# Casts and sigmoids placed behind bank copies, another order at the entry of the feed-forward stage, and 20 instead of 16 pairs in seven products

## The reference

```python
    x = x + merged @ wo
    h = rmsnorm(x, g_ffn)
    a, u = jnp.split(h @ w_gu, 2, axis=-1)
    return x + (jax.nn.silu(a) * u) @ w_dn
```

## Time and profile before

| | us |
|---|---|
| median of 3 runs | 1005.48 (1004.69 to 1010.24) |
| profiled execution, its time | 1006.62 |
| its span in the profile | 1004.5 |
| TensorE busy | 952.2 |
| VectorE busy | 602.9 |
| ScalarE busy | 403.2 |
| feed-forward stage, first product to last | 580.8 to 992.5 |

### The profile page before, as it was taken

How to read it: one execution, slowest core, us unless ns; L and a number is a source line. 1 busy time by engine, 2 the same in 40 slices (tenths; PEclk the granted TensorE clock), 3 DMA queues, 4 the chain that set the end, 5 groups by cost and what they waited for, 6 DMA issues and landing times. The chain is left out here.

```text
span 1004.5 us, 18642 instructions
## 1 busy us (share of the span) xinstructions
PE 952.2 (95%) x7431; PEld 926.3 (92%) x7431; DVE 602.9 (60%) x1167; ACT 403.2 (40%) x746; POOL 77.4 (8%) x107
## 2 busy tenths in 40 slices
PE   6999999999999899999999988999999899999997
PEld 5899989999988898999999977999999899999997
DVE  5745465445985661735355768876448776447653
ACT  7343234444553441422223545454225444225453
POOL 0100023011202000202031000000000000000000
PEclk9999999999999999999999979999999999999999
DMA  8783237322312774232222331524212313221302
GB/s 238 177 235 44 45 89 178 101 76 77 104 47 71 202 197 134 76 94 85 84 85 79 119 136 43 209 74 135 86 43 84 126 44 127 84 85 47 106 19 89
DMA packets 104912, 104.78 MB, mean 104 GB/s; under 512 B 11130, under 2 KB 101752, under 8 KB 104492
## 3 DMA queue, kind: packets, MB, share of 16 engines
q1 hardware_dynamic: 101224, 92.51, 30.9%
q0 software_dynamic: 3552, 11.08, 4.0%
q10 hardware_dynamic: 52, 0.01, 0.0%
HBM read 97.74 MB, written 15.45 MB: 113 GB/s over the span
## 5 line engine op out<-in xcount | busy, mean ns | idle before, releaser
L651 PE MATMUL acc<-h_hi,w_hi 128*128 128x288 f32 (+1 forms) x816 | 256.9, 315 | 3.1 <-DVE w_lo L634 2.1
L651 PE MATMUL acc<-h_lo,w_hi 128*128 128x288 f32 (+1 forms) x816 | 234.8, 288 | 0.0
L651 PE MATMUL acc<-h_hi,w_lo 128*128 128x288 f32 (+1 forms) x800 | 229.9, 287 | 0.0
L651 PEld LDWEIGHTS acc<-h_hi,w_hi 128*128 128x128 f32 x816 | 153.8, 188 | 11.7 <-issue 4.9
L651 PEld LDWEIGHTS acc<-h_lo,w_hi 128*128 128x128 f32 x816 | 154.0, 189 | 4.1 <-issue 2.4
L651 PEld LDWEIGHTS acc<-h_hi,w_lo 128*128 128x128 f32 x800 | 150.5, 188 | 0.0
L1366 PE MATMUL acc<-h_hi,w_hi 128*128 128x272 f32 x440 | 129.7, 295 | 15.5 <-ACT acc L1803 15.4
L624 ACT ACTIVATE w_hi<-raw 128x1024 fp32r<-128x1024 f32 (+1 forms) x67 | 70.5, 1052 | 166.1 <-PE acc L651 165.3
L1366 PE MATMUL acc<-h_lo,w_hi 128*128 128x272 f32 x440 | 128.8, 293 | 0.0
L1366 PE MATMUL acc<-h_hi,w_lo 128*128 128x272 f32 x440 | 128.7, 293 | 0.0
L1781 ACT ACTIVATE w_hi<-raw 128x512 fp32r<-128x512 f32 (+1 forms) x105 | 64.8, 621 | 97.5 <-PE acc L1366 91.9
(11 more groups left out here) (401 smaller groups left out, 1999.1 us busy)
## 6 DMA issues: line engine op xcount, KB each, us to landing
raw<-in_w_in SPq DMA_DIRECT2D x25, 1024.0 KB, 5.6
raw<-in_w_gate_up SPq DMA_DIRECT2D x22, 1024.0 KB, 5.2
raw<-in_w_down SPq DMA_DIRECT2D x8, 1024.0 KB, 5.3
rev<-tab POOLq DMA_DIRECT2D x1, 4352.0 KB, 20.2
ring<-in_cache_dsa_kv SPq DMA_DIRECT2D x4, 1024.0 KB, 7.8
raw<-in_w_out SPq DMA_DIRECT2D x4, 1024.0 KB, 5.8
out<-in_cache_dsa_kv SPq DMA_DIRECT2D x2, 2016.0 KB
ring<-in_cache_moba_k SPq DMA_DIRECT2D x48, 64.0 KB, 2.6
```

The source lines that it names most:

```text
L651: ins = nc.tensor.matmul(acc[:, bank, 0:HALF[half]], a[:, k, :], two(b[:, kx + k, :], half), start=first and k == k0 and c == 0, stop=last ...
```

## The change

- Of the 22 gate and up pairs only the first and the last stay in the eight-product form: 20 instead of 16 are in the seven-product form, pairs 1 to 8, 13 to 20 and 25 to 28.
- The sigmoids of a seven-form gate pair come at 3.1 products behind it in ScalarE's queue (1.8 before), those of pair 0 at 1.2; the casts of a seven-form up pair at 4.2 and 4.45 (1.5 and 1.75), their low parts on VectorE 0.8 behind; the gate multiplies at 3.7 (3.6).
- At the entry: the second norm's matmuls at product 9 instead of 2, its roots at 9.5 instead of 2.5, its reciprocal at 10.5 instead of 3.1, `over_rms` from 14.5 instead of 8.5 on. The high and low parts of h for q = 2 are made in two halves, the slots 4 to 7 later, and the sums and slots 4 to 7 of q = 3 later too. The first six weight operands have times of their own (`EARLY`).

```diff
-        EIGHT = (0, 4, 8, 13, 17, 21)
+        EIGHT = (0, 21)
...
-        RING, LEAD = 6, 5
+        RING = 6
+        EARLY = (n_wout - 1.6, n_wout - 1.55, n_wout - 0.95, n_wout - 0.9, n_wout + 1, n_wout + 1.75)
...
-            return tm(last_use[operands[u - RING]] + 1) if u >= RING else tm(u - LEAD) if u >= 4 else n_wout - 0.94 + 0.05 * u
+            return tm(last_use[operands[u - RING]] + 1) if u >= RING else EARLY[u]
...
-        T_SIG, T_GATE = 1.8, 3.6
+        T_SIG, T_GATE = 3.1, 3.7
...
-            return q + 1 if q < 3 else 4 + min(slot // 2, 2) if q == 3 else 6 + 2 * (q - 4) + (1 if slot < 2 else 2)
+            first = {0: (1, 1, 1), 1: (2, 2, 2), 2: (3, 3, 6), 3: (4, 5, 7)}
+            return first[q][min(slot // 2, 2)] if q < 4 else 7 + 2 * (q - 4) + (1 if slot < 2 else 2)
...
-            return lag(n, 1.5 + 0.25 * m_) if n in seven else tm(evac_time[n, "12" if m_ == 0 else "22"] + 0.3)
+            return lag(n, 4.2 + 0.25 * m_) if n in seven else tm(evac_time[n, "12" if m_ == 0 else "22"] + 0.3)
...
                 def second_norm():
-                    yield tm(2)
+                    yield tm(9)
...
-                    for q in range(3):
+                    for q in range(2):
                         yield n_merge + 2 * q + 2.5
                         act.wait_ge(sem("b_sum"), 4 * q + 4)
                         b_his(q, slice(0, 8), h8_hi[:, q])
+                    yield n_merge + 6.5
+                    act.wait_ge(sem("hs_done"), 6)
+                    b_his(2, slice(0, 4), h8_hi[:, 2])
...
-                    yield n_wout + 0.6
+                    act.wait_ge(sem("b_sum"), 12)
+                    b_his(2, slice(4, 8), h8_hi[:, 2])
+                    yield tm(4.5)
                     act.wait_ge(sem("b_sum"), 16)
                     b_his(3, slice(4, 8), h8_hi[:, 3])
...
-                            yield lag(n, T_SIG)
+                            yield lag(n, T_SIG if n in seven else 1.2)
...
                 def feed():
-                    yield tm(2.5)
+                    yield tm(9.5)
...
                 def results():
-                    yield tm(3.1)
+                    yield tm(10.5)
...
                 def over_rms():
-                    yield tm(6)
+                    yield tm(12)
...
-                        yield tm(8.5 + 2 * k)
+                        yield tm(14.5 + 2 * k)
```

More of the change, by code:

```diff
@@ L1747, in merge @@
                             act.wait_ge(b_lo, 2 * KD + k // 2)
+                            act.wait_ge(sem("b_sum"), 2 * k)
                         nc.scalar.activation(s_tile[:, k % 2, :], xT[:, k, :], ACT.Copy, scale=vecs[:, 8 + k:9 + k]).then_inc(sem("hs_done"), 1)
@@ L1995, in b_low, with t_sums @@
                                             ALU.subtract).then_inc(b_lo, 1)
+                def t_sums(q):
+                    b_sum(4, 1, 0, "b_sum")
+                    b_sum(6, 2, 0, "b_sum")
+                    dve.wait_ge(sem("b_sum"), 4 * q + 1)
+                    b_sum(5, 2, 4, "b_sum")
+                    dve.wait_ge(sem("b_sum"), 4 * q + 3)
+                    b_sum(7, 5, 3, "b_sum")
                 def h_parts():
@@ L2001, in h_parts @@
                         dve.wait_ge(sem("hs_done"), 2 * q + 2)
-                        b_sum(4, 1, 0, "b_sum")
-                        b_sum(6, 2, 0, "b_sum")
-                        dve.wait_ge(sem("b_sum"), 4 * q + 1)
-                        b_sum(5, 2, 4, "b_sum")
-                        dve.wait_ge(sem("b_sum"), 4 * q + 3)
-                        b_sum(7, 5, 3, "b_sum")
+                        t_sums(q)
                         yield n_merge + 2 * q + 2.7
                         dve.wait_ge(b_hi, 2 * KD + q + 1)
-                        b_low(slice(0, 8), h8_hi[:, q], h8_lo[:, q])
-                    hi, lo = h8_hi[:, 3], h8_lo[:, 3]
+                        slots = slice(0, 8 if q < 2 else 4)
+                        b_low(slots, h8_hi[:, q], h8_lo[:, q])
                     yield n_wout - 0.4
                     dve.wait_ge(b_hi, 2 * KD + 4)
-                    b_low(slice(0, 2), hi, lo)
+                    b_low(slice(0, 2), h8_hi[:, 3], h8_lo[:, 3])
                     yield n_wout + 0.01
                     dve.wait_ge(b_hi, 2 * KD + 5)
-                    b_low(slice(2, 4), hi, lo)
-                    yield n_wout + 0.5
-                    dve.wait_ge(sem("hs_done"), KD)
-                    b_sum(4, 1, 0, "b_sum")
-                    b_sum(6, 2, 0, "b_sum")
-                    dve.wait_ge(sem("b_sum"), 13)
-                    b_sum(5, 2, 4, "b_sum")
-                    dve.wait_ge(sem("b_sum"), 15)
-                    b_sum(7, 5, 3, "b_sum")
-                    yield n_wout + 0.9
-                    dve.wait_ge(b_hi, 2 * KD + 6)
-                    b_low(slice(4, 8), hi, lo)
+                    b_low(slice(2, 4), h8_hi[:, 3], h8_lo[:, 3])
+                    yield tm(2)
+                    dve.wait_ge(b_hi, 2 * KD + 6)
+                    b_low(slice(4, 8), h8_hi[:, 2], h8_lo[:, 2])
+                    yield tm(3)
+                    dve.wait_ge(b_lo, 2 * KD + 6)
+                    t_sums(3)
+                    yield tm(6)
+                    dve.wait_ge(b_hi, 2 * KD + 7)
+                    b_low(slice(4, 8), h8_hi[:, 3], h8_lo[:, 3])
                 def w_sums():
@@ L2076, in results @@
                             if kind == "up":
-                                dve.wait_ge(b_lo, 2 * KD + 6 + 2 * j)
+                                dve.wait_ge(b_lo, 2 * KD + 7 + 2 * j)
                                 dve.wait_ge(sem("t_done"), 2 * j + 2)
@@ L2134, in gated_up @@
                                 yield part_time(n, m) + 0.25 * 0.8
-                                dve.wait_ge(b_hi, 2 * KD + 6 + 2 * j + m + 1)
+                                dve.wait_ge(b_hi, 2 * KD + 7 + 2 * j + m + 1)
                                 b_low(slice(2 * m, 2 * m + 2), s4_hi[:, j - FIRST[c]], s4_lo[:, j - FIRST[c]])
```

## The result

| | before | changed |
|---|---|---|
| median, timed together (us) | 1007.79 | 977.43 (976.57 to 980.58) |
| ratio, 95% interval | 1 | 0.9706 (0.9665 to 0.9747) |
| profiled execution: time, span | 1006.62, 1004.5 | 977.73, 975.9 |
| feed-forward stage, from its first matmul to the first one behind it | 580.8 to 992.4 | 581.4 to 963.4 |

The change takes 29.6 us away by the ratio (0.0294 x 1007.79), 28.9 by the two profiled executions. The forecast was 975, with 966 to 989 as its range. All of it lies in the feed-forward stage, which is 29.6 us shorter (the 992.5 of the table of before is the end of the last matmul, 992.4 the start of the next one, as it is taken for the changed kernel); it starts 0.6 later, and what follows it takes 0.3 more, which leaves the 28.6 of the spans.

The account below looks back on a forecast made before the run. TensorE was taken as the bound, losing time to late bank copies and at the feed-forward entry; 6.0 (fewer matmuls) + 20.2 (order) + 4.4 (entry) = 30.6 us off the median 1005.48 gave 975, forecast 970 to 983, wider range 966 to 989.

Parts of the forecast that it names:

- The bound: Whole kernel: TensorE, busy 95% of the span, sets the time; undisturbed matmuls take 0.1256 us each.
- Four more pairs: 6.0 us: Gate and up pairs: four more in seven-product form save 48 matmuls, 6.0 us, all on TensorE's path.
- The order: 20.2 us, 1.7 left: Seven-form pairs: later sigmoids and casts free the bank copies, gaining 20.2 of 21.9 us lost, 1.7 left.
- the walk's margin of 0.4 us: Step-by-step timing of one seven-form pair: result "22" at 4.15, product 4 needs it at 4.53, 0.4 us to spare.
- The fourth block: First down pair of a chunk: low part ready after about 1.05 us, fourth block read after 1.13: no loss.
- The entry: 4.4 us: Feed-forward start: later norm ends pair 0 at 595.0 and pair 1 at 611.9 against 616.3, gaining 4.4 us.
- the half clock behind the pause: Pair 1, after a pause of 6.1 us: TensorE at half clock loses 3.0 us, as after the 4.44 us one.
- The table load: ScalarE before pair 0's sigmoids: 1.28 us load covered by waiting; with the skill page's drain the entry would give 3.5.
- VectorE behind, 988: Rival, seven-form pairs: VectorE's waits make a pair 11.4 us, 14.5 us lost, gain 17.8, time 988; chance 0.18.
- The slower side, 1037: Rival, seven-form pairs: gate multiplies waiting for late sigmoids delay "22" and product 4, 63.4 us lost, 1037; chance 0.03.
- The entry without gain: Rival at the entry: pair 1 waits until 610 anyway or half clock eats the gain, 979.5; chance 0.09.
- the entry with a short pause: Rival at the entry: pause in pair 1 below 2 us, some 5 us more, 970 or 968; chance 0.10.

Follow-up runs that it names:

- Experiment 2: Kernel before with only the times of sigmoids, casts and gate multiplies of seven-form pairs changed (3.1, 4.2, 3.7): 986.0 us, ratio 0.9788.
- experiment 12: Changed kernel with gate multiplies at 3.2 and the xT multiplies moved into the first down pairs (73.2 on, 0.6 apart): 974.92 us, ratio 0.9654.
- experiment 10: Changed kernel with gate multiplies at 3.2 and the xT multiplies at 20.5 + 3k instead of 14.5 + 2k: 977.18 us, ratio 0.9686.
- experiment 6: Changed kernel with pair 0's sigmoids at 4.1 instead of 1.2, behind pair 1's copies, and its gate multiplies at 4.4: 981.3 us, ratio 0.9724.
- experiment 7: Changed kernel with the edits of experiment 5 and experiment 6 together: 978.51 us, ratio 0.97.
- experiment 9: experiment 7 with the norm's reciprocal at 16.45 instead of 10.5 and the xT multiplies from 20.5 on, three products apart: 978.55 us, ratio 0.9709.
- experiment 1: Kernel before with only the 20 seven-form pairs, old order and old entry kept: 1031.15 us, ratio 1.0225.
- experiment 3: Changed kernel's entry alone, with 16 seven-form pairs and the old times of casts, sigmoids and gate multiplies: 1003.65 us, ratio 0.9949.
- experiment 5: Changed kernel with VectorE's gate multiplies at 3.2 instead of 3.7: 976.25 us, ratio 0.9678.

## Why the prediction was right, and where its terms were off

**The bound.** TensorE at a pace of 0.1256 us per matmul, and losses found by comparing pairs with that pace: right. Down pairs still take 12.05 us each, undisturbed seven-form pairs 10.57. The division as written, 48.30 / 384, gives 0.1258; the four pairs run from 702.94 to 751.16, 48.22 us, and that gives 0.1256.

**Four more pairs: 6.0 us.** Right as a count. Experiment 2 beside the changed kernel shows 3.4 net of the new waits, some of which belong to the entry.

**The order: 20.2 us, 1.7 left.** 21.4 alone (experiment 2); in the changed kernel 4.4 us are left over the pace from pair 2 on and not 1.7. From pair 2 on the stage is 23.5 us shorter (376.1 to 352.6), for 6.0 + 20.2 = 26.2. What is left has three places. Product 4 of pair 3 loses 1.13 by late VectorE, foreseen as 1. Seven times (at product 4 in pairs 1, 5, 7, 15, 17, 19 and 27) the walk's margin of 0.4 us was missing, 0.35 each and 0.5 in the first, 2.6 in all. Three things ate it: VectorE's wait for its own gate multiply (0.28 from start to start, left out); product 4's turn, which comes 4.36 us after the end of product 5 and not 4.53, since the next product starts before the last one ends; and 0.15 from the end of "22" to the start of the matmul that waits for it. And where a down pair follows a seven-form pair (pairs 9 and 21), put at nothing, 0.27 are lost each time: the low part is ready 1.27 us after the start of the down pair at 687.08 and not 1.05, so the tenth matmul comes at 688.41 where 688.21 is its turn, and TensorE restarts slowly. The fourth block was priced with 0.08 us to spare, too little to call it nothing.

**The entry: 4.4 us.** The start of pair 2 moved from 35.5 to 29.4 us after the start of the stage: 6.1. Step by step: end of pair 0 at 595.8 (595.0, where the stage itself starts 0.6 later); the rounding behind the root done at 594.56 (594.2); reciprocal done at 598.75 (598.4); sigmoids 603.26 (602.75); product 6 at 604.85 (604.4); pause 5.87 (6.1). The term that was mis-sized is the half clock behind the pause, taken as 3.0 us from the 4.44 us wait before. It cost 1.4: product 6 took 2.86 for 1.51, and from 608 on the clock was 1.00. I had put the longer pause nearer to the costlier of two rows; the length of a pause does not order them: behind pauses of 5.3 us 2.4 (experiment 12) and 2.7 us (experiment 10) were lost. That the entry gave more than 4.4 was luck in this execution.

**The table load.** In the changed kernel it runs from 601.36 to 602.64 and is covered, as in the walk: the sigmoids start at 603.26, and what they wait for is VectorE. In experiments 6, 7, 9, 10 and 12 nothing covers it; in 10 and 12, without the multiply of xT, the pause ends by it, since the results of pair 0 are done 0.05 us before the load is. ScalarE in experiment 9:

```profile
606.93 1.28 ACT L1826 ACT_TABLE_LOAD   x1
608.23 1.20 ACT L1826 ACTIVATE sq<-ga 128x544 f32<-128x544 f32 x2
```

The sigmoids start 0.02 us behind the load, as the root did before, and the load starts 0.01 us behind the rounding ahead of it (606.29, 0.63 us long). The Trainium skill (ScalarE: Activation LUTs, "What ACT_TABLE_LOAD costs") adds about 1.38 us of drain to a load of 1.283; the traces agree with the load and show no drain on either side of it.

**The sum.** Errors of -2.7 in the steady part and +1.7 at the entry, with a stage that starts 0.6 later and a tail 0.3 longer: 28.6 us off the span where 30.6 were forecast. That the total lies so near is helped by luck: the two errors have opposite signs.

**The rivals.** VectorE behind, 988: not in the changed kernel, but close; two additions of 0.6 us per pair make 990.73 of it. The slower side, 1037: its mechanism, waits of product 4 for "22" behind the gate multiplies, is where the 0.35 us are lost, in every second pair, where it decides at 1.9 in each; but it was not the late sigmoids that made "22" late. Its price per pair, 3.73 us from the worst window, was met in experiment 1 by the old copy waits, 3.6 to 4.1 in ten of seventeen pairs. The entry without gain and the entry with a short pause both fell; none of the orders tried in experiments 6, 7 and 9 gives the second.

## What to carry to other kernels

In a queue that runs in order, look at what an instruction has ahead of it and what that waits for, not at how busy its engine is: ScalarE was 40% busy and cost TensorE 22 us, and moving two casts or two sigmoids of a pair behind three copies gave back 21.4. Cut the trace at the starts of the tile pairs and compare with the undisturbed pace, since the waits named in a list (15.4 us) are less than what they cost (21.9, and 50.9 for 29.4 in experiment 1). Price a change together with the one that makes room for it: the longer runs of seven-form pairs lose 22.7 us alone, and behind the new order, with the new entry, pairs 2 and later take 3.4 less.

## What the runs showed of the hardware that was not expected

- A wait of 1.95 us of TensorE costs 2.2 us or 3.7: in windows of like pairs the granted clock is 1.00 in some (12.74 us before, pairs 6 and 14; 12.73 to 12.75 in experiment 1) and 0.88 in others (14.28 before; 14.27 in experiment 1; 14.27 in experiment 3). When such waits come in each pair, most are of the costly kind: ten of the fourteen in experiment 1.
- Half clock behind a pause of nearly the same length lasted 3 us (5.87, changed kernel) or 5.1 us (5.26, experiment 12). In the changed kernel's four timed executions the longest span (978.6) has the lowest mean clock (0.991), the others (974.6 to 975.9) have 0.995 and 0.996. That the scatter between executions comes from this is likely, and not shown, since only one of each is profiled.
- VectorE waits 0.20 us for its own last result where a semaphore stands between the two, 0.28 from start to start; one independent instruction in between hides that (experiment 5).
- A matmul that starts late by only 0.28 us costs 0.35, because the next one starts 0.20 us behind it and not 0.125 (769.06 in the changed kernel).
